# Order of the partial products in the SSD and mLSTM sums, and the place of a store and reload on SyncE's queue, in a two-layer hybrid encoder

## The reference

```
h = rmsnorm(x);  [attention | SSD | mLSTM inputs] = h @ W_in        # 1024 x 2848
x = x + concat(window_attention, ssd, mlstm) @ W_out
x = x + expert_choice_swiglu_moe(rmsnorm(x))                         # 16 experts
# SSD, per chunk of 128 rows, forward and backward:
y = (C B^T * exp(segsum(a))) @ (x dt)      # inside the chunk
  + (C @ state_before) * exp(cumsum a)     # from earlier chunks
# mLSTM, per chunk, forward and backward: the same two parts
num = (exp(dmat - m) * (q k^T)) @ v + (q @ C_before) * sc
```

## Time and profile before

| | |
|---|---|
| runs, us | 2274.96, 2276.5, 2277.64 (median 2276.5) |
| profiled execution | 2274.96 us, span 2273.5 us |
| TensorE busy | 2225.7 us, 98% of the span, 12446 matmul records |
| VectorE, ScalarE, GpSimd busy | 1246.9, 606.0, 565.9 us |
| mean granted clock | 0.997 of full speed |
| SSD loop, layer 0 | about 232 to 389 us |
| mLSTM loop, layer 0 | about 435 to 502 us |

### The profile page before, as it was taken

One profiled execution on the slowest core, in us unless ns is written; L12 is line 12 of the kernel. 1 busy time (PEld: TensorE's weight loads), 2 busy tenths in 40 slices (PEclk: granted clock), 3 DMA queues, 4 the chain that ended last, 5 costly groups with the idle time before them and its releaser, 6 DMA issues.

```text
span 2273.5 us, 32428 instructions
## 1 busy us (share of the span) xinstructions
PE 2225.7 (98%) x12446; PEld 1575.3 (69%) x12446; DVE 1246.9 (55%) x2427; ACT 606.0 (27%) x1397; POOL 565.9 (25%) x658
## 2 busy tenths in 40 slices
PE   8999999999999999999999999999999999999998
PEld 6557578874446888887775565888744468887786
DVE  3554466587766344555236544665876654555442
ACT  3221233374332111111132212334733321111111
POOL 1103454154311111111111044541443121111111
PEclk9999999999999999999999999999999999999999
DMA  4002122533648988878530111334336589878883
GB/s 158 21 20 73 57 93 95 151 121 102 200 154 286 343 301 285 293 265 288 143 131 22 37 56 56 111 114 109 112 117 206 171 292 339 300 269 283 294 291 79
DMA packets 179540, 388.84 MB, mean 171 GB/s; under 512 B 12181, under 2 KB 63897, under 8 KB 179386
## 3 DMA queue, kind: packets, MB, share of 16 engines
q1 hardware_dynamic: 164122, 344.82, 43.9%
q0 software_dynamic: 15264, 41.95, 7.5%
HBM read 329.77 MB, written 56.96 MB: 170 GB/s over the span
## 4 chain that ended last, share of the span: by engine, by line
PE 87%; DVE 7%; ACT 3%; DMA 1%; issue 1%; POOL 1%; SPq 0%; DVEq 0%; ACTq 0%; POOLq 0%
PE ps L1962 85%; DVE TMP L1774 1%; ACT SCR L1126 1%; DVE TMP L1330 1%; DVE HT L1904 1%; PE ps L1981 1%; DVE SCR L1779 1%; DMA HT<-h_sample,idxs 0%; DVE TMP L1779 0%; PE ps L2014 0%; POOL SCR L818 0%; DVE HT L1330 0%; DVE SCR L1652 0%; DVE TMP L1339 0%; DMA MID<-w_in 0%
## 5 line engine op out<-in xcount | busy, mean ns | idle before, releaser
L1962 PE MATMUL ps<-MID,HT 128*128 128x512 f32 (+3 forms) x2560 | 685.5, 491 | 6.1 <-DMA MID<-w_in 3.6
L1962 PEld LDWEIGHTS ps<-HT,MID 128*128 128x128 f32 x4096 | 556.4, 191 | 16.7 <-issue 15.6
L1962 PE MATMUL ps<-HT,MID 128*128 128x160 f32 (+1 forms) x4096 | 559.7, 299 | 1.3 <-DVE HT L1330 1.3
L1962 PEld LDWEIGHTS ps<-MID,HT 128*128 128x128 f32 (+1 forms) x2560 | 298.7, 157 | 288.3 <-issue 245.3
L1962 PE MATMUL ps<-RING,HT 128*128 128x256 f32 (+2 forms) x1760 | 394.3, 392 | 2.8 <-DVE RING L1334 2.0
L1962 PEld LDWEIGHTS ps<-RING,HT 128*128 128x128 f32 (+1 forms) x1760 | 310.9, 190 | 71.8 <-issue 30.5
L1962 PE MATMUL ps<-HT,RING 128*128 128x512 f32 (+1 forms) x960 | 349.7, 522 | 0.0
L1962 PEld LDWEIGHTS ps<-HT,RING 128*128 128x128 f32 x960 | 180.2, 190 | 153.3 <-issue 145.2
L1904 DVE STREAM_TRANSPOSE HT<-HT 32x256 f32<-32x256 f32 x576 | 251.1, 436 | 18.4
L1339 DVE SCALAR_TENSOR_TENSOR HT<-HT,ps 128x160 f32<-128x160 f32 (+1 forms) x128 | 40.8, 319 | 396.6 <-ACT HT L1292 394.6
L925 POOL DMA_INDIRECT y_prompt<-SCR,idxp x32 | 50.3, 1573 | 583.7 <-ACT SCR L1302 562.8
(11 more groups left out here) (281 smaller groups left out, 2104.4 us busy)
## 6 DMA issues: line engine op xcount, KB each, us to landing
MID<-w_gate SPq DMA_DIRECT2D x32, 2048.0 KB
MID<-w_up SPq DMA_DIRECT2D x32, 2048.0 KB
MID<-w_down SPq DMA_DIRECT2D x32, 2048.0 KB
RING<-w_in SPq DMA_DIRECT2D x20, 1024.0 KB, 5.3
SCR<-cs_rows SPq DMA_DIRECT2D x20, 1024.0 KB, 5.1
p_rows<-SCR SPq DMA_DIRECT2D x12, 768.0 KB
HT<-p_rows SPq DMA_DIRECT2D x48, 192.0 KB, 3.5
y_sample<-RING SPq DMA_DIRECT2D x16, 512.0 KB, 4.8
```

The source lines that it names most:

```text
L1962: return pe.matmul(out, a, b, start=start, stop=stop)
```

## The change

In `ssd_sum` and `ml_sum` the diagonal part is issued first and the off part last; both waits stand ahead of all matmuls. In SyncE's list the store of `XS` moves up, ahead of `m_load(0)`, together with its wait for `y_done`. The reload moves down, behind `m_load(2)`.

```diff
                     sp.wait_ge(scratch_stored, 48)
                     sp.wait_ge(y_made, NC)
+                    sp.wait_ge(y_done, NC)
+                    for c in (0, NC // 2):
+                        sp.dma_start(yrr[c * P:(c + NC // 2) * P, :].rearrange("(c t) w -> t c w", t=P), XS[:, c:c + NC // 2]).then_inc(scratch_stored, 16)
                     wo_rows = wo[layer * D:(layer + 1) * D, :].rearrange("(k p) n -> p k n", p=P)
                     for c in range(NC):
                         m_load(c)
-                        if c == 1:
-                            sp.wait_ge(y_done, NC)
-                            for h in (0, NC // 2):
-                                sp.dma_start(yrr[h * P:(h + NC // 2) * P, :].rearrange("(c t) w -> t c w", t=P), XS[:, h:h + NC // 2]).then_inc(scratch_stored, 16)
+                        if c == 2:
                             sp.wait_ge(scratch_stored, 80)
                             for b in range(4):
                                 sp.dma_start(XSF[32 * b:32 * b + 32, :].rearrange("p (c a w) -> p c a w", c=NC, a=4),
...
                     def ssd_sum(c):
                         t = tcol(c)
+                        pe.wait_ge(w_made, 2 * (c + 1))
                         if c >= 1:
                             pe.wait_ge(y_read, c)
+                        for h in range(SH):
+                            mm(ps[:, 5, h * HD:(h + 1) * HD], DM[:, c % 2, 0, h * P:(h + 1) * P], XS[:, c, h * HD:(h + 1) * HD])
                         for g in range(2):
-                            mm(ps[:, 6 + g, :].rearrange("p (d n) -> p d n", d=2), BC[64 * g:64 * g + 64, 1, t:t + P],
-                               PREV[64 * g:64 * g + 64, :, c, :])
-                        pe.wait_ge(w_made, 2 * (c + 1))
-                        for h in range(SH):
-                            last = mm(ps[:, 5, h * HD:(h + 1) * HD], DM[:, c % 2, 0, h * P:(h + 1) * P], XS[:, c, h * HD:(h + 1) * HD])
+                            last = mm(ps[:, 6 + g, :].rearrange("p (d n) -> p d n", d=2), BC[64 * g:64 * g + 64, 1, t:t + P],
+                                      PREV[64 * g:64 * g + 64, :, c, :])
                         last.then_inc(y_made, 1)
...
                     def ml_sum(c):
+                        pe.wait_ge(mw_made, 2 * c + 2)
                         if c >= 1:
                             pe.wait_ge(nd_read, c)
+                        for d in range(2):
+                            for h in range(MH):
+                                mm(ps[:, 5 + d, 65 * h:65 * h + 65], DMM[c % 3][:, d, h, :], V[:, c, h, :])
                         for j in range(2):
                             for q in range(2):
                                 b = 64 * q
                                 out = ps[:, 4 + 3 * q, 0:260].rearrange("p (d j e) -> p d j e", d=2, j=2)[:, :, j, :]
-                                mm(out, QK[b:b + 64, j, c * P:(c + 1) * P], PREVM[b:b + 64, :, c, j, :])
-                        pe.wait_ge(mw_made, 2 * c + 2)
-                        for d in range(2):
-                            for h in range(MH):
-                                last = mm(ps[:, 5 + d, 65 * h:65 * h + 65], DMM[c % 3][:, d, h, :], V[:, c, h, :])
+                                last = mm(out, QK[b:b + 64, j, c * P:(c + 1) * P], PREVM[b:b + 64, :, c, j, :])
                         last.then_inc(nd_made, 1)
```

## The result

The change is slower: 2303.75 us (median of four, 2300.83 to 2308.15) against 2276.17 us for the kernel before, a ratio of 1.0122 with an interval of 1.0105 to 1.014. That is 27.6 us more, twice the 13.8 that I forecast, and above my range of 2283 to 2297. The profiled execution took 2302.91 us, with a span of 2301.4 us (27.9 more).

A forecast was written before the change was run, and what follows sets the result against it. The prediction took TensorE's own instruction list as the bound. Order 11.3 us plus reload 2.5, store 0, made 13.8 on the profiled 2274.96: 2288.8, or 2290.3 us as a median, with a range of 2283 to 2297.

The forecast's parts named there:

- What bounds the kernel: Whole kernel: TensorE's own list bounds it, busy 2225.7 of 2273.5 us; other engines' waits count only where TensorE meets them.
- Edit 1, the order: Sums in both loops: two blocks of 64-row matmuls instead of one cost 0.34 us a chunk, 11.3 us in all.
- the gain at the last SSD chunk: Last SSD chunk, without next products: the off part is dearer to enter from a unit; the new order gains 0.13 us.
- the loss absorbed at the last mLSTM chunk: Last mLSTM chunk: TensorE waits for VectorE before the off part in the old order, so 0.34 us are absorbed.
- Edit 2, the store: Store of XS ahead of the first two row loads: cost 0, their delay hidden by 38 us of mLSTM states.
- Edit 3, the reload: Reload behind m_load(2) in the mLSTM loop: m_load(3) lands late; 2.4 us in layer 0, 0 in layer 1, taken as 2.5.
- From the landing to TensorE: mLSTM loop: late m_load(3) delays ScalarE, then VectorE's last release; TensorE's chunk 3 stalls, about 2 us in layer 0, lie inside.
- the reload costs much: Rival, mLSTM loop: m_load(4) late too, ScalarE loses time in each of chunks 3 to 6; 8 us or more, chance 0.12.
- The reload costs nothing: Rival, mLSTM loop: DMAs share the engines, so the moved reload is free and only the order costs; 2287.8 us, chance 0.10.
- Weight loads hidden: Rival, both loops: weight loads run ahead across row changes, leaving drains of 0.18 us a chunk; 2285 us, chance 0.07.
- absorbed: Rival, both loops: another chain than TensorE's sets the pace and absorbs delays; result within 0.2%, chance 0.06.
- faster: Rival, both loops: row changes beside the short-stream diagonal part cost nothing, hiding weight loads; 2272.6 us, chance 0.03.

The follow-up runs named there:

- the run with a queue of its own: The changed kernel with the row loads of chunks 3 and 4 taken out of SyncE's list and issued from ScalarE's queue: 2302.86 us, ratio 1.0116.

## Why the prediction was wrong

- **What bounds the kernel**: right. Both losses are TensorE's.
- **Edit 1, the order**: right, in its parts too. 3.41 us from products to unit, periods of 13.96 and 6.87, 2.96 and 2.63 us a layer (2.95 and 2.69), 11.2 of 11.3 us in all. The 3.45 that I wrote for products to unit is a slip: 0.05 of it is the unit's own, and without that my terms give 3.41. That the gain at the last SSD chunk and the loss absorbed at the last mLSTM chunk were taken from the two timelines gave the last tenths.
- **Edit 2, the store**: the mechanism of its cost was right (none), but a gain of 0.86 us a layer was missed. I had asked who waits for the moved row loads, and not what runs beside the masks that they release.
- **Edit 3, the reload: the step that failed**, 14.8 us in place of 2.5. The mechanism, `m_load(3)` late behind the reload, was right, and GpSimd's mask did wait for it (21 us, some 15 written). But "it lands at about 456 in layer 0 and 453.7 in layer 1", 21.2 and 18.9 us into the loop, was 27.3 and 21.2 (464.65 and 1609.90, in loops that start at 437.38 and 1588.69). Of this, "I take it that one queue serves in order" is false: W_out, issued behind the load, took some 4 us of it in layer 0. And "13 us of reload", read from an idle stretch, had the reload done by 452; its last piece landed at 457.8, 20.0 us after the first was issued, where the kernel before took 15.4. The 2 to 4 us that I had allowed as a bound did not cover 6.1.
- **From the landing to TensorE**: I followed the delay down ScalarE's list to the last chunk and held TensorE's own stall at chunk 3 for part of it, some 2 us. But TensorE comes to the products of chunk 4 at 25.5 us of the loop and can run them only 5.9 us after the mask of chunk 3 starts, and nothing gives that back. With the 21.2 that I had written for layer 0 this is a stall of 1.6 us. Each microsecond by which the load came later lengthened it by one, and with 27.3 it is the measured 7.6, which is 5.2 more than the 2.4 that I counted there. In layer 1 the two idles, 1.55 and 0.84, make nearly all of the 2.5, where I counted 0.
- **The clock**: not in the sum at all. 4.6 us in layer 0. With the 5.2 and the 2.5 this is the 12.3 us between edit 3 as written and as measured.
- **Elsewhere** 3.6 us more, of which no edit is shown to be the cause: 2.5 at the layer border, at half clock again (above), and 0.8 just ahead of the experts of layer 0, where the other traces differ by -1.6 to +1.8 us from the kernel before. Why they do stays open.
- **The rivals**: "the reload costs much", to which I had given 0.12, came nearest, but 2303.75 is above its own 2296 to 2302, and its mechanism is not what happened. ScalarE doesn't lose time in each of chunks 3 to 6: TensorE has one stall at chunk 3 and a slow stretch behind it, and from 482.01 us on the period is 6.87 again. "The reload costs nothing" fell with the stall. "Weight loads hidden", "absorbed" and "faster" fell with the 13.96 us of the period.

Not tried: whether work for TensorE during the stall would keep the clock. By the program and the trace all eight PSUM banks are held at that point (two units that ScalarE has yet to copy out, the products of chunk 3 and the sum of chunk 2 that VectorE has yet to read), so that there is nowhere for such matmuls to write. The clock's share is therefore read from rows at either level and not from a kernel without it.

## What to carry to other kernels

Ask of a moved transfer not how long it took where the engines were idle, but which small load will now be in flight together with it, in front of it and behind it: a row load of 512 KB behind 2.6 MB, a table of 768 KB and in front of 1 MB came 6 us later than a sum of durations said, and four pieces between the row loads cost nothing. A stall of the bounding engine has a second price: here every one of 2.6 us or more was followed by 4.3 to 5.4 us lost at half clock, so two layers with shorter stalls can cost more than one with a long stall (4.59 and 3.04 us cost 17.2 in the run with a queue of its own, 7.62 and 1.55 cost 14.8 in the change). And matmuls that use part of the array belong in one block; it is the number of blocks that costs, 0.34 us for each further one here, not their place.

## What the runs showed of the hardware

- A second block of 64-row matmuls costs 0.34 us, in the SSD loop (4 records of 512 columns) as in the mLSTM loop (8 of 130); the same matmuls in one block, placed elsewhere, 0.
- Four DMAs of 640 KB in pieces of 512 B held SyncE for 9.6 us while they were issued, and the next DMA for 4.3 us. Alone in the gap of the SSD stage they held it for 7.8.
- Of two row loads of equal size with full engines, the one on a queue of its own landed 11.4 us after its issue and the one on the shared queue 12.5.
- On one queue a row load of 512 KB landed at 464.46 us, after three DMAs of 256 KB that were issued 1.5 to 2.6 us behind it. With the 1 MB of which they are a part moved away, its mask started some 4 us sooner.
- Behind TensorE's stalls of 2.6 to 8.2 us the granted clock was 0.50 for 6.8 to 13.7 us; behind those of 0.94 and 1.55 us it stayed at 1.00.
- Five operations of VectorE with two inputs in SBUF took 2.91 us beside GpSimd's masks and 2.13 us without them. The Trainium skill ("GPSIMD Engine Reference", Specifications) says that the two engines share their SBUF interfaces and contend in such operations; the rows agree.
